# The opening norm of a decoder trunk done tile by tile, with two more pairs of weight tiles, a new order of its first loads, and one sum of w_o moved up by a tile

## What is computed

```python
mod = (silu(c) @ ada_w[l] + ada_b[l]).reshape(bsz, 3, 3, 1024)       # shift, scale, gate of 3 sub-layers
h = rmsnorm(x) * norm_gain[l] * (1 + mod[:, 0, 1]) + mod[:, 0, 0]
x = x + 0.5 * (1 + mod[:, 0, 2]) * (silu(h @ w1) * (h @ w3)) @ w2    # 1024 -> 2816 -> 1024
...                                                                  # h from x again
mixed = g0 * (ya @ w_rg) + g1 * (yb @ w_sb) + g2 * (yc @ w_fox)
x = x + (1 + mod[:, 1, 2]) * (mixed @ w_o)
...                                                                  # second feed-forward as the first
```

## Time and profile before

| | |
|---|---|
| median of 3 runs | 2769.68 us (2768.7 to 2770.67) |
| the profiled execution | 2768.65 us, of which the span in the profile is 2766.9 us |
| granted TensorE clock | 0.994 of full |
| TensorE busy | 2683.0 us, 97% of the span |
| DVE, ACT, POOL busy | 1288.2, 1060.9, 1163.0 us |
| moved | 323.82 MB, mean 117 GB/s |

### The profile page before, as it was taken

How to read it: one execution, slowest core, us unless ns; L and a number is a source line. 1 busy time by engine, 2 the same in 40 slices (tenths; PEclk the granted TensorE clock), 3 DMA queues, 4 the chain that set the end, 5 groups by cost and what they waited for, 6 DMA issues and landing times.

```text
span 2766.9 us, 31911 instructions
## 1 busy us (share of the span) xinstructions
PE 2683.0 (97%) x13172; PEld 2247.2 (81%) x13172; DVE 1288.2 (47%) x1612; ACT 1060.9 (38%) x1598; POOL 1163.0 (42%) x468
## 2 busy tenths in 40 slices
PE   3999999999999999999999999999999999999998
PEld 3888888878888878888888888888788888888887
DVE  6566337875543143511056663478545422453111
ACT  5232227654344244222252232566444442523223
POOL 2555444432223434545435554354223234345442
PEclk9999999999999999999999999999999999999999
DMA  5655533221112323523245554322112122253322
GB/s 222 213 183 198 175 123 104 89 73 61 62 61 69 99 85 130 179 95 99 96 141 189 201 190 162 102 92 89 64 61 69 62 77 95 82 189 123 102 97 76
DMA packets 90833, 323.82 MB, mean 117 GB/s; under 512 B 10048, under 2 KB 12480, under 8 KB 90432
## 3 DMA queue, kind: packets, MB, share of 16 engines
q1 hardware_dynamic: 90688, 321.78, 34.1%
HBM read 319.64 MB, written 2.10 MB: 116 GB/s over the span
## 4 chain that ended last, share of the span: by engine, by line
PE 88%; DVE 6%; ACT 4%; issue 1%; POOL 1%; DMA 0%; SPq 0%; ACTq 0%; DVEq 0%
PE bank L1277 27%; PE bank L1276 27%; PE bank L1275 27%; PE bank L1310 2%; PE bank L1426 1%; PE bank L1315 1%; DVE e_lo L1101 1%; DVE e_hi L1099 1%; PE bank L1459 1%; DVE e_f L1094 1%; POOL w_lo L448 1%; DVE ada L1175 1%; DVE gt L1001 1%; ACT w_hi L478 1%; PE bank L1473 1%
## 5 line engine op out<-in xcount | busy, mean ns | idle before, releaser
L448 POOL TENSOR_TENSOR w_lo<-raw,w_hi 128x1024 fp32r<-128x1024 f32 x440 | 1142.8, 2608 | 1491.1 <-ACT w_hi L478 1490.7
L1275 PE MATMUL bank<-h_hi,w_hi 128*128 128x512 f32 x2240 | 876.5, 391 | 9.5 <-POOL w_lo L448 9.5
L1276 PE MATMUL bank<-h_lo,w_hi 128*128 128x512 f32 x2240 | 874.2, 390 | 0.0
L1277 PE MATMUL bank<-h_hi,w_lo 128*128 128x512 f32 x2240 | 874.1, 390 | 0.0
L478 ACT ACTIVATE w_hi<-raw 128x1024 fp32r<-128x1024 f32 x440 | 464.2, 1057 | 972.9 <-PE bank L1277 901.5
L1275 PEld LDWEIGHTS bank<-h_hi,w_hi 128*128 128x128 f32 x2240 | 421.8, 188 | 98.2 <-issue 10.2
L1277 PEld LDWEIGHTS bank<-h_hi,w_lo 128*128 128x128 f32 x2240 | 421.5, 188 | 88.5
L1276 PEld LDWEIGHTS bank<-h_lo,w_hi 128*128 128x128 f32 x2240 | 421.8, 188 | 87.4
L845 DVE CUSTOM_DVE_ANT_0 ada<-ada,c_act 128x1024 f32<-128x1024 f32 x144 | 284.0, 1979 | 238.6 <-DMA ada<-ada_w 238.3
L1277 PE MATMUL bank<-g_hi,w_lo 128*128 128x512 f32 (+1 forms) x792 | 295.2, 373 | 0.0
L1276 PE MATMUL bank<-g_lo,w_hi 128*128 128x512 f32 (+1 forms) x792 | 292.3, 369 | 0.0
(11 more groups left out here) (212 smaller groups left out, 3005.6 us busy)
## 6 DMA issues: line engine op xcount, KB each, us to landing
raw<-w_units SPq DMA_DIRECT2D x440, 512.0 KB, 3.5
ada<-ada_w SPq DMA_DIRECT2D x144, 512.0 KB, 4.8
ada<-ada_w SPq DMA_DIRECT2D x8, 1024.0 KB, 16.6
x<-x_in SPq DMA_DIRECT2D x4, 512.0 KB, 6.7
wab_raw<-wab SPq DMA_DIRECT2D x2, 1024.0 KB, 5.7
y<-fin SPq DMA_DIRECT2D x8, 256.0 KB, 2.1
c_act<-c_rows SPq DMA_DIRECT2D x1, 512.0 KB, 3.8
vec<-vecs SPq DMA_DIRECT2D x3, 92.5 KB, 3.6
```

The costliest lines, as they stand in the source:

```text
L448: nc.gpsimd.tensor_tensor(w_lo[s][:, :, :], raw[u % RAW][:, :, :], w_hi[s][:, :, :].bitcast(F32), ALU.subtract).then_inc(unit_lo.sem, 1)
L1275: nc.tensor.matmul(o, wh, xh, start=start, stop=False, skip_group_check=True)
L1276: nc.tensor.matmul(o, wh, xl, start=False, stop=False, skip_group_check=True)
L1277: return nc.tensor.matmul(o, wl, xh, start=False, stop=stop, skip_group_check=True)
```

## The change

The change rewrites what lies between the first load and the third hidden tile, and moves one statement in the mixer.

1. Loads: x comes ahead of the vectors, with a semaphore for each of its four transfers. ada_w's first 16 tiles are reordered so that each 1 MB transfer brings the shift tile k and the scale tile k, and units 0 to 3 follow the first four of them one by one; units 2 and 3 have raw buffers of their own (`raw0`). Units 4 and 5 are loaded behind the last ada transfer.
2. silu(c) is copied by ACT to two neighbouring PSUM banks (`bank45`), and the 16 first ada products take it from there.
3. The norm is no longer in halves: one sum of 512 columns, one Ln, one Exp (rstd now in SBUF), x times rstd on POOL (`first_xr`) instead of DVE, shift and scale of tile k made by two 128x1 operations on ACT (`first_h` of ACT), then h_hi and the unrounded h of 512 columns, in bank 6 or 7.
4. TensorE's `first_h` takes tile k for units 0 and 1 as it comes, and for units 2 and 3 from behind tile 3 on.
5. Units 4 and 5 (`EXTRA`) have tiles of their own, `wx_hi` and `wx_lo`, so they need not wait for the ring.
6. The mixer's constants are rounded on ACT behind the norm.
7. w_o: `sum_squares(l, 1, 0)` stands between the second halves of tiles 6 and 7.

```diff
+            for u in range(RING):
+                first_ada(u)
+                if u < RAW:
+                    sp.dma_start(raw[u][:, :, :], w_units[u]).then_inc(raw_loaded[u].sem, 16)
+                else:
+                    sp.dma_start(raw0[u - RAW][:, :, :], w_units[u]).then_inc(raw0_loaded[u - RAW].sem, 16)
+            for g in range(RING, KD):
+                first_ada(g)
+            for u in EXTRA:
+                load_unit(0, u)
...
+            def first_xr(k):
+                if k >= 2:
+                    gp.wait_ge(hf_0.sem, k - 1)
+                nc.gpsimd.tensor_tensor(tmp[k % 2][:, :], x[:, k, :], rstd[:, :], ALU.mult).then_inc(xr_0.sem, 1)
...
+            def first_h(k):
+                shift, scale = mod[:, k:k + 1], nscale[:, 0, k:k + 1]
+                act.wait_ge(ada_done.sem, G0 * k + 2)
+                A(shift, shift, ACT.Identity, bias=vec[:, V_ADAB + k:V_ADAB + k + 1]).then_inc(mod_0.sem, 1)
+                A(scale, mod[:, KD + k:KD + k + 1], ACT.Identity, bias=spc[:, 5, k:k + 1],
+                  scale=vec[:, V_NORM1 + k:V_NORM1 + k + 1]).then_inc(mod_0.sem, 1)
+                act.wait_ge(mod_0.sem, 2 * k + 2)
+                act.wait_ge(xr_0.sem, k + 1)
+                A(h_hi[:, k, :], tmp[k % 2][:, :], ACT.Identity, bias=shift, scale=scale).then_inc(hh_0.sem, 1)
+                if k >= 2:
+                    act.wait_ge(hl_0.sem, k - 1)
+                A(bank[6 + k % 2][:, :], tmp[k % 2][:, :], ACT.Identity, bias=shift, scale=scale).then_inc(hf_0.sem, 1)
...
+            for k in range(KD):
+                first_h(k)
+                if k in (1, 2, 5, 6):
+                    first_tick({1: 2, 2: 3, 5: 4, 6: 5}[k])
...
+            def first_ada(k):
+                dve.wait_ge(ada0_loaded[k].sem, 16)
+                for i in range(G0):
+                    V.tensor_tensor_reduce(ada0[k][:, i, :], ada0[k][:, i, :], bank45[:, :], 1.0, 0.0, ALU.mult,
+                                           ALU.add, mod[:, KD * i + k:KD * i + k + 1]).then_inc(ada_done.sem, 1)
...
+                    for k in range(4):
+                        first_h(k, (0, 1))
+                    first_h(0, (2, 3))
+                    first_h(1, (2, 3))
+                    for k in range(4, KD):
+                        first_h(k, (0, 1))
+                        first_h(k - 2, (2, 3))
+                    for k in range(KD - 2, KD):
+                        first_h(k, (2, 3))
...
-                sum_squares(l, 1, 0)
+                        if h == 1 and n == KD - 2:
+                            sum_squares(l, 1, 0)
```

More of the change, by code:

```diff
@@ L128 @@
 SQ_BASE = {-1: -8, 0: 0, 1: 8, 2: 17}
+EXTRA = (RING, RING + 1)
 def X_AT(m, n, h=None):
@@ new lines, in _ @@
+            for n in range(KD):
+                if n % 2 == 0:
+                    act.wait_ge(x_loaded[n // 2].sem, 16)
+                if n >= 3:
+                    act.wait_ge(sqsum_0.sem, n - 2)
+                A((tmp[n % 2] if n else sqsum)[:, :], x[:, n, :], ACT.Square).then_inc(sq_0.sem, 1)
+            nc.scalar.preload_act_table_set("natural_log_exp_and_others")
+            first_tick(0)
+            act.wait_ge(cols_set.sem, 2)
+            act.wait_ge(sumsq_0.sem, 1)
+            A(rstd[:, :], bank[BS][:, :], ACT.Ln, bias=eps_col[:, 0:1], scale=1.0 / D).then_inc(ln_0.sem, 1)
@@ L734, in _ @@
[L734 to L740, removed]
             for l in range(DEPTH):
-                if l == 0:
-                    h_round(l, -1, 0, 0, {2: lambda: tick(l, 0)})
-                else:
+                if l:
                     h_round(l, -1, 0, 0, {0: lambda: tick(l - 1, UNITS - 1), 3: lambda: square(l - 1, 2, KD - 1, 1),
@@ new lines, in first_rest @@
+            def first_rest(k):
+                dve.wait_ge(hf_0.sem, k + 1)
+                V.tensor_tensor(h_lo[:, k, :], bank[6 + k % 2][:, :], h_hi[:, k, :].bitcast(F32),
+                                ALU.subtract).then_inc(hl_0.sem, 1)
+            for n in range(1, KD):
+                dve.wait_ge(sq_0.sem, n + 1)
+                if n > 1:
+                    dve.wait_ge(sqsum_0.sem, n - 1)
+                V.tensor_tensor(sqsum[:, :], sqsum[:, :], tmp[n % 2][:, :], ALU.add).then_inc(sqsum_0.sem, 1)
@@ new lines, in _ @@
+            dve.wait_ge(vec_loaded.sem, 16)
+            V.scalar_tensor_tensor(out=spc[:, 5, :], in0=vec[:, V_ADAB + KD:V_ADAB + 2 * KD], scalar=1.0,
+                                   in1=vec[:, V_NORM1:V_NORM1 + KD], op0=ALU.add, op1=ALU.mult).then_inc(gb_0.sem, 1)
+            dve.wait_ge(silu_c.sem, 1)
+            dve.wait_ge(c_wide.sem, 1)
+            first_ada(0)
+            for k in range(1, KD):
+                first_ada(k)
+                first_rest(k - 1)
+            first_rest(KD - 1)
@@ L1289, in pair @@
                 pe.wait_ge(unit_lo.sem, unit_lo.at(l, u + 2))
+                if l == 0 and u in EXTRA:
+                    tiles = [(wx_hi[j], wx_lo[j]) for j in range(2)]
+                else:
+                    tiles = [(w_hi[(u + j) % RING], w_lo[(u + j) % RING]) for j in range(2)]
                 for k in range(KD):
@@ L1292, in pair @@
                         pe.wait_ge(ready.sem, ready.at(l, k + 1))
[L1293 to L1295 removed]
+                    for (wh, wl), b in zip(tiles, (b0, b1)):
+                        i = mm3(bank[b][:, :], wh[:, k, :], wl[:, k, :], hi[:, k, :], lo[:, k, :], k == 0,
                                 k == KD - 1)
@@ L1535, in w_rg @@
                 unit(l, U_WRG(n), bank[7][:, :], ya_hi, ya_lo)
-            pe.wait_ge(consts_v.sem, 10)
-            sum_squares(0, -1, 0)
+            pe.wait_ge(ones_set.sem, 1)
+            pe.wait_ge(sqsum_0.sem, KD - 1)
+            nc.tensor.matmul(bank[BS][:, :], ones_r[:, :].bitcast(F32), sqsum[:, :], start=True, stop=True,
+                             skip_group_check=True).then_inc(sumsq_0.sem, 1)
             for l in range(DEPTH):
```

178 lines of the change are left out of this document (118 added, 60 removed).

## The result

| | before | after |
|---|---|---|
| median of runs side by side | 2770.18 us (2768.70 to 2770.74, 4 runs) | 2738.73 us (2738.04 to 2739.48, 4 runs) |
| profiled execution / its span | 2768.65 / 2766.9 us | 2738.97 / 2737.2 us |
| granted TensorE clock | 0.994 | 0.994 |

The ratio of after to before is 0.9887, with a 95% interval of 0.9872 to 0.9903. Forecast were 2740.5 us, with a range of 2737 to 2748.

A forecast was written before the change was run, and what follows sets the result against it. TensorE bounds the kernel, busy 2683.0 of 2766.9 us; DVE bounds the opening. Opening 23.6 plus w_o 5.5 gives 29.1 us off 2768.65, 2739.6; as that execution stands 1.0 below the median, forecast 2740.5, range 2737 to 2748.

The forecast's parts named there:

- T: Opening: time at which the pair of units 4 and 5 starts on TensorE; forecast 49.5 us, against 73.10 before.
- The sum of 512 columns: Opening's norm: the sum of squares as one matmul on an idle TensorE, taken as 2.0 us and hidden.
- POOL's product: Opening: x times rstd for one tile, 128x512, on POOL, taken as 1.25 us, bounds 0.74 and 3.6.
- DVE's product with silu(c) from PSUM: Opening: each ada product on DVE stays at 1.22 us while POOL works, bounds 1.2 and 3.35.
- the rival had said 63.9 and 2755: Opening: PSUM doesn't save DVE from POOL, nine products take 3.35 us, T = 63.9, time 2755; chance 6%.
- Tile 3 to T: Opening: from 30.6 us TensorE always has work, 78 matmuls at 0.227 us, 17.7 us, units ending at 48.3.
- h_lo of tile 7: End of the opening's units: TensorE waits some 0.6 us for it, moving their end from 48.3 to 48.9.
- the 50.2 with the clock: Opening: T if TensorE enters the stretch from tile 3 at half clock, losing 1.9 us, without waiting for h_lo.
- rival of half clock again and again: Opening: TensorE's bursts with waits keep the clock low until some 8 us into the unbroken stretch; T 52, 2743 us; 13%.
- The wait for units 4 and 5: Behind the opening: the 2.4 us wait for w_lo goes, as both units are ready at 44.5, 5 us to spare.
- No new wait: After T: pair 6, 7 has its remainders at about 55, needed at 60.4, so no wait at 55 to 75 us.
- w_o: Moved sum: next feed-forward starts 2.74 us earlier in each of two layers, together 5.5 us, bounds 0 and 5.8.

The follow-up runs named there:

- Experiment 2: The kernel after, with the 16 first ada products reading silu(c) from SBUF again: 2750.26 us, 0.9926 of before.
- experiment 5: The kernel before, with the first 16 ada products reading silu(c) from PSUM and one ACT copy added: 2766.59 us, 0.9984 of before.
- experiment 4: The kernel before, with the sum of w_o moved and nothing else: 2762.39 us, 0.9973 of before.
- Experiment 6: The kernel after, with own tiles for the fifth and sixth unit of all four feed-forwards: 2729.52 us, 0.9851 of before.
- experiment 3: The kernel after, with units 4 and 5 rounded into the ring, without tiles of their own: 2741.60 us, 0.9896 of before.

## Why the prediction was right, point by point

**T.** Forecast 49.5, measured 49.43. The rounds of ACT show it step by step (timeline after):
```profile
19.66 0.81 ACT L561 ACTIVATE h_hi<-tmp,mod,nscale 128x512 fp32r<-128x512 f32 x1
...
22.94 0.81 ACT L561 ACTIVATE h_hi<-tmp,mod,nscale 128x512 fp32r<-128x512 f32 x1 [1.29 <-POOL tmp L502]
...
29.20 0.81 ACT L561 ACTIVATE h_hi<-tmp,mod,nscale 128x512 fp32r<-128x512 f32 x1 [0.37 <-POOL tmp L502]
...
37.98 1.06 ACT L551 ACTIVATE wx_hi<-raw 128x1024 fp32r<-128x1024 f32 x1 [1.69 <-DMA raw<-w_units]
...
42.50 0.81 ACT L561 ACTIVATE h_hi<-tmp,mod,nscale 128x512 fp32r<-128x512 f32 x1
```

| h_hi of tile ready at | 0 | 1 | 2 | 3 | 4 | 5 | 6 | 7 |
|---|---|---|---|---|---|---|---|---|
| forecast | 21.2 | 24.4 | 27.4 | 30.6 | 34.2 | 36.1 | 40.3 | 43.3 |
| measured | 20.5 | 23.8 | 26.7 | 30.0 | 33.6 | 35.6 | 40.3 | 43.3 |

Up to tile 5 it is 0.5 to 0.7 early, as unit 0 is (it landed by 14.27, forecast 15.0); from tile 6 on, where ACT waits for unit 4's load at 38.0, as forecast, they agree.

**The terms without a row.** The sum of 512 columns took 2.05 us (taken 2.0, bounds 1.2 to 2.4). It began at 13.71, 0.6 later than forecast, and was not quite hidden, for ACT's Ln waited 0.52 us for it; but rstd was there at 17.20, before POOL was through with the remainder of unit 0 (17.76), so nothing hung on it. POOL's product took 1.27 us, its line in the timeline:
```profile
17.73 1.27 POOL L502 TENSOR_TENSOR tmp<-x,rstd 128x512 f32<-128x512 f32 x1
```
Taken were 1.25, between 0.74 and 3.6; the choice rested on DVE being out of the way. DVE's product with silu(c) from PSUM took 1.215 us (taken 1.22, between 1.2 and 3.35), and the last one was done at 40.1 (forecast 41). Experiment 2 shows what the wrong choice would have cost, T = 61.8 and 2750; the rival had said 63.9 and 2755, some 2 us too much since not as many products were fully held (median 1.86 us) as the nine that I had counted.

The row of 88 multiplies with one operand in PSUM was the right one to read this from. The Trainium skill (SBUF — State Buffer, the section "Who interferes with whom") has the mechanism: DVE with two operands in SBUF and GpSimd reading SBUF contend for one shared port pair, and the one that comes second is blocked until the first's instruction ends. By that rule experiment 5's addition of 16 columns must end with POOL's remainder, and the trace agrees within 0.03 us.

**Tile 3 to T.** Forecast 17.7 us for 78 matmuls and 0.6 of waiting or 1.9 for the clock. Measured were 49.43 - 30.07 = 19.4, so 1.7 more than 78 distances; 0.4 of it are two waits for h_lo (0.21 and 0.18), the rest are short gaps where a tile's first matmul comes a little late. The 0.6 us that I had for h_lo of tile 7 was 0.2: it was done at 44.71, as forecast, and the three distances from 44.42 to 45.33 took 0.91 us instead of 0.68. Against the 48.9 that I had without the clock, two small errors partly cancelled: tile 3 came 0.5 earlier, and the stretch behind it was 1.1 longer than 17.7 and 0.6. The other 0.5 was met by my step half-way to the 50.2 with the clock, but no half clock came into this stretch. The mechanism of T was right; that it came out within 0.1 us was luck.

**The half clock.** The rival of half clock again and again had 13%, T = 52. TensorE did begin at 1.2 GHz, as forecast; it was at 2.4 GHz from 24.82 on, before its short waits were over. What it cost lies in the first 4.3 us, where TensorE would have waited for the next tile anyway. The rule of the Trainium skill that I had set against the change (TensorE: Matmul & The Clock Gate, the section on HAM oscillation) did not decide here: the wait of 0.35 us came before the clock had risen, and those of 0.83 and 1.17 us between the next bursts did not bring the low clock back. The kernel that the page describes waits longer than that for its loads. In experiment 2, where TensorE waited up to 2.65 us in the opening, the low clock did come back (0.51 in 36 to 43 us), so the rival was not baseless; it was the products from PSUM that kept the waits short.

**The wait for units 4 and 5** went, 5 us ahead of need: the second remainder was done at 44.5, as forecast. **No new wait** came at 55 to 75 us. The constants on ACT (43.93 to 45.38) were hidden.

**w_o.** Forecast 2.74 per layer. At the first matmul of the next feed-forward it is 1028.49 - 1002.57 - 23.30 = 2.62, a little less, for the 24 matmuls and the sum took 3.30 us and not the 3.18 that I had summed. At the next common stop, 29 us on, it is 2.88: the four units behind the norm took 28.66 us instead of 28.92, without the wait in front of them. The first matmul behind that wait had taken 0.39 us where it now takes 0.28; what else makes up the 0.26 I did not trace. The mechanism was right, the term 5% too small.

The total, 31.5 us by the medians and 29.7 by the profiled spans, against 29.1, is right within what separates two executions. In the spans the surplus is 0.6, which is what the granted clock left at the two places of layer 1 named above; in the medians it is 2.4, and no run says where that lies. Of my conditions for being wrong (DVE's products stretch, POOL's product over 2 us, a slower queue, a new wait) none came about.

## What to carry to other kernels

Before a norm or any other prologue is spread tile by tile, list which operands DVE reads from SBUF in pairs while POOL works: here one copy of 1.03 us into PSUM was worth 12 of the 23.7 us, but alone in the old order only 3 to 5, since the next operation with two SBUF operands took over the stall, however small it was. Forecast a serial start by the times at which its inputs land and one engine's order, and count the unbroken matmuls behind the last late input; here every tile of h was forecast within 0.7 us that way, while the 0.1 us at the end was luck. When a stall is found behind one of four alike stages, look at the other three: the same own tiles were worth 2.3 us in the first and, applied to all, another 9, of which 7.1 are the waits themselves.

## What was unexpected in the hardware

**A wait of 2.4 us sometimes costs half a clock.** The kernel has waits of 2.4 us behind which the granted clock drops, and the same waits without it. Windows of 50 us in the trace before, with the columns of experiment 2:
```profile
50.00:100.00 50.00, 47.62 (x291) 42.75 (x290) 30.29 (x45) 25.77 (x41) 19.21 (x9) 1.00 0.43 149
...
1400.00:1450.00 50.00, 47.45 (x296) 42.95 (x295) 29.62 (x49) 26.94 (x45) 19.80 (x8) 0.97 0.52 176
```
The same two in experiment 4, which is the same program up to there:
```profile
50.00:100.00 50.00, 47.63 (x282) 42.86 (x281) 28.49 (x44) 26.15 (x43) 18.78 (x8) 0.97 0.43 148
...
1400.00:1450.00 50.00, 47.44 (x305) 43.16 (x305) 29.19 (x50) 28.30 (x47) 19.37 (x9) 1.00 0.52 180
```
The drop has changed places between two executions of the same instructions. In the trace before, three of the four waits for a w_lo have a window of 0.97 (at 1057, 1427 and 2412 us), and after it is two of three (1031 and 2382, not 1401). At 0.97 over 50 us it is 1.5 us of clock each, which is the size of the scatter of these kernels. Experiment 6 took three such waits away and won 2.1 us more than their length. Behind the waits of 4.3 us for k_lo (550 to 600 and 1900 to 1950) the windows showed 0.90 to 0.93 in the traces before, after and of experiments 4 and 6, but 0.97 at the first of them in experiment 2 and at the second in experiment 3.

**The first pair of the kernel after runs a little slower.** The 48 matmuls of pair 4, 5 took 60.67 - 49.43 = 11.24 us, 0.234 each, where the steady distance is 0.227. That is 0.3 us, and its cause stays open. In the kernel before, the 17 distances from 73.40 to 77.30 us are 0.229 each, so it is only in small part the same there.
